# Recurrence products of 64x64 cut into 32x32, and their compact results half as wide

## The chip, the cores and the metric

The kernel runs on one NeuronCore of a Trainium2 chip (trn2). The metric is the device time of one execution in microseconds, here the median of three runs. The engines are TensorE (PE in the profile, its weight loads PEld), VectorE (DVE), ScalarE (ACT), GpSimd (POOL) and SyncE (SP, which issues the DMAs of the weights).

## What is computed

Two blocks of a network on 256 tokens of width 2048 in float32: a convolution mixer, a gated linear recurrence (HGRN2), sliding window attention and a SwiGLU. The change touches the recurrence alone. For each of 16 heads of 128 channels and for both directions it computes, with `b` the running sum of the log forget gates:

```
diff = b[:, :, :, None, :] - b[:, :, None, :, :]
decay = jnp.exp(jnp.where(lower_tri, diff, -jnp.inf))
scores = jnp.einsum("bhtk,bhsk,bhtsk->bhts", qb, kb, decay)
o_intra = jnp.einsum("bhts,bhsv->bhtv", scores, vb)
```

The decay depends on query, key and channel, so the scores aren't one matrix product.

## The kernel before

All large products are three passes in fp32r (high part times high part and two cross terms, lines 508 to 510). Weights stream through four slots: SP loads a chunk of 256x512, ACT rounds it (`w_hi`, L761), DVE or POOL computes the rest (`w_lo`, L1146), PE multiplies 12 times. A tick is one chunk on each engine, and the other work is hooked behind ticks by hand (`Hooks`). Every engine runs its list strictly in order; semaphores join them (`g_mm` counts PE's levels, `g_G` the finished operands, `g_S` the taken results).

The recurrence splits the 256x256 score matrix of a head into a diagonal and off-diagonal squares of halving size: `LEVELS = [64, 32, 16, 8, 4, 2, 1]`. Within one square the decay factors into a part of the query and a part of the key relative to a boundary between them, so a level is an ordinary product of two scaled operands. Four heads form a group (`j` = 0 to 3), and there are nine steps `s`: 0 the diagonal, 1 the square of 128, 2 to 8 the seven levels. For each step:

- `diffs` (DVE, lines 1355 to 1358) writes the exponents to `E`, `exp` (ACT, L959) takes their exponential, `weigh` (DVE, L1366) multiplies by the query;
- `level` (PE) multiplies. Before, it computes for each of four heads and two token blocks two 64x64 squares on the diagonal of a 128x128 block, and in step 2 the two squares beside it. In steps 3 to 8 most of a 64x64 square is not wanted: the squares of the level lie inside it;
- `take` gets the wanted entries out of PSUM (`T`) into SBUF: `SB` is a compact array of the squares, `ST` the full 128x128 blocks. Steps 0 to 3 are taken by ACT, 4 to 8 by DVE with a copy under the mask `lmask` (L1375).

At the end `blocks` (ACT, L988) puts `SB` into the diagonal of `ST`, and `av` (PE, lines 624 and 625) multiplies the scores by the values. PE runs the steps of group `j` between the chunks of the next weights: step 0 after tick 8, step 1 after 13, step `s` after 10 + 2 s, `av` after 28. DVE and ACT have their parts of them one tick later, which is earlier in time, since they run ahead of PE. After the last step of a group DVE transposes the next group's gates in quarters, POOL moves the quarters (L448, `kf`, `kb`, `qT`), ACT makes gates of them.

Of the kernel before, what the change touches and what calls it, by code (L numbers as in the profile page):

```python
# [29 lines left out]
I32 = mybir.dt.int32  # L30
ACT = mybir.ActivationFunctionType
# [3 lines left out]
P = 128  # L35
D = 2048
S = 256
# [12 lines left out]
HPG = GC // P  # L50
# [7 lines left out]
LEVELS = [64, 32, 16, 8, 4, 2, 1]  # L58
TWO_PI = 2 * np.pi
QUARTER = P // 4  # L60
LN_MIN = 2.0 ** -64
FIRST_LOWS = 2 * CPG
ACT_TAKES = 4
HB = P // 2
# [68 lines left out]
def is_first(j):  # L133
    return isinstance(j, int) and j == 0
# [19 lines left out]
def build(nc, t, out):  # L154
    ph = phases()
    ctx = ExitStack()
    with ctx:
        def sb(stack, name, shape, dt=F32):
            return stack.enter_context(nc.sbuf_tensor(name, shape, dt))

        def sem(name):
            return ctx.enter_context(nc.semaphore(name))
# [19 lines left out]
        mix = ExitStack()  # L182
        y_hi = sb(mix, "y_hi", [P, KT, S], F32R)
        ones = sb(mix, "ones", [P, P])
        lmask = sb(mix, "lmask", [P, len(LEVELS) + 2 - ACT_TAKES, P // 2], I32)
        wmask = sb(mix, "wmask", [P, 3 * P])
        inv_freq = sb(mix, "inv_freq", [P, HD // 2])
        onorm = sb(mix, "onorm", [P, P])
# [21 lines left out]
        hs = ExitStack()  # L210
# [7 lines left out]
        qT = sb(hs, "qT", [P, HPG, S])  # L218
# [3 lines left out]
        Xc = sb(hs, "Xc", [P, HPG, S])  # L222
        E = sb(hs, "E", [P, 2, 2, HPG, S])
        ST = sb(hs, "ST", [P, 2, HPG, 2, P])
        SB = sb(hs, "SB", [P, HPG, 2, P // 2])
        back = sb(hs, "back", [P, 2, HPG])
        ssh = sb(hs, "ssh", [P, 3, 2 * HPG])
        powers = sb(hs, "powers", [P, 2 * HPG])
# [29 lines left out]
        T = ctx.enter_context(nc.psum_tensor("T", [P, 4, 512], F32))  # L258
# [3 lines left out]
        def gate_banks(k):  # L262
# [17 lines left out]
        g_raw, g_q, g_M, g_act, g_lb, g_D, g_E, g_G, g_mm, g_S = (  # L280
            sem(f"hgrn_{s}") for s in ("raw", "quarters", "moved", "act", "lb", "D", "E", "G", "mm", "S"))
# [202 lines left out]
        def _(pe):  # L484
# [48 lines left out]
            def v_turn(j):  # L533
                if is_first(j):
                    pe.wait_ge(small_in, 16)
                pe.wait_ge(c_v, j + 1)
                if not is_first(j):
                    pe.wait_ge(c_pad, 2 * j)
                transposes(T01, atok, c_T)
# [43 lines left out]
            at = Hooks().put(4, lambda: v_turn(3))  # L583
# [11 lines left out]
            def level(j, s):  # L595

                pe.wait_ge(g_G, 9 * j + s + 1)
                if s == 0:
                    pe.wait_ge(g_M, 3 * j + 3)
                if s >= 2:  # L600
                    pe.wait_ge(g_S, 9 * j + s - 1)
                e = E[:, (s + 1) % 2, :, :, :]
                for h in range(HPG):
                    for b in range(2):
                        if s == 1:
                            last = nc.tensor.matmul(T[:, h // 2, (h % 2) * S + b * P:(h % 2) * S + b * P + P],
                                                    e[:, 0, h, b * P:(b + 1) * P], e[:, 1, h, (1 - b) * P:(2 - b) * P],
                                                    start=True, stop=True)
                            continue
                        for i in range(2):  # L610
                            at = (2 * b + i) * HB
                            to = (2 * b + 1 - i) * HB if s == 2 else at
                            g, q = (e[:, 1, h, at:at + HB], qT[:, h, to:to + HB]) if s == 0 else (e[:, 0, h, at:at + HB], e[:, 1, h, to:to + HB])
                            last = nc.tensor.matmul(T[i * HB:(i + 1) * HB, 2 + s % 2, (2 * h + b) * HB:(2 * h + b + 1) * HB],
                                                    g, q, start=True, stop=True)
                last.then_inc(g_mm, 1)

# [10 lines left out]
            def process(j):  # L628

                at = Hooks().put(8, lambda: level(j, 0))  # L630
                for s in range(1, 9):
                    at.put(13 if s == 1 else 10 + 2 * s, lambda s=s: level(j, s))
                return at.put(28, lambda: av(j))
# [18 lines left out]
            at = process(3)  # L652
# [59 lines left out]
            at = Hooks().put(14, k_turn)  # L712
            for g in range(4):
                e = 16 + 8 * g
# [23 lines left out]
        def _(act):  # L738
            A = nc.scalar.activation
# [84 lines left out]
            def v_steps(j):  # L824
                return Hooks().put(2, lambda: b_out(j)).put(4 if j < 2 else 6, lambda: pad_copy(j))
# [25 lines left out]
            def z_out(k):  # L851
                if k:
                    act.wait_ge(c_zT, k)
                evacuate("conv_z", 0, k, 0, sg, ACT.Silu, c_z)

            def z_copy(k):
                act.wait_ge(c_zT, k + 1)
                for b in range(2):
                    A(szt[:, 4 * k + 2 * b:4 * k + 2 * b + 2, :].rearrange("p a b -> p (a b)"), T[:, b, :],
                      ACT.Copy).then_inc(c_zc, 1)  # L860
# [20 lines left out]
            def ln_act(u):  # L881
                act.wait_ge(c_n, u + 1)
                for kt in (2 * u, 2 * u + 1):
                    last = A(cy[:, kt, :], cy[:, kt, :], ACT.Silu, scale=feat[:, kt, R_LNG:R_LNG + 1], bias=feat[:, kt, R_LNB:R_LNB + 1])
                last.then_inc(c_act, 1)
# [5 lines left out]
            at = v_steps(3)  # L891
# [8 lines left out]
            at = Hooks().put(0, lambda: ln_act(0)).put(3, lambda: z_out(3)).put(5, lambda: z_copy(3))  # L900
# [60 lines left out]
            def take(j, s):  # L961

                act.wait_ge(g_mm, 9 * j + s + 1)
                if s == 0:
                    A(SB[:, :, :, :].rearrange("p a b c -> p (a b c)"), T[:, 2, :], ACT.Copy).then_inc(g_S, 1)
                    return
                if s == 1:
                    if not is_first(j):
                        act.wait_ge(g_av, j)
                    A(ST[:, 0, :, :, :].rearrange("p a b c -> p (a b c)"), flat(T01), ACT.Copy).then_inc(g_S, 1)  # L970
                    return
                c = LEVELS[s - 2]
                ps = T[:, 2 + s % 2, :].rearrange("p (a c) -> p a c", c=HB)
                for i in range(P // c):
                    r, o = slice(i * c, (i + 1) * c), (i ^ 1) * c
                    if s == 2:
                        last = A(ST[r, 1, :, :, o:o + c].rearrange("p a b c -> p (a b) c"), ps[r, :, :], ACT.Copy)
                    else:
                        o = o % HB
                        last = A(SB[r, :, :, o:o + c].rearrange("p a b c -> p (a b) c"), ps[r, :, o:o + c], ACT.Copy)  # L980
                last.then_inc(g_S, 1)

            def blocks(j):

                act.wait_ge(g_S, 9 * j + 9)
                for i in range(2):
                    r = slice(i * HB, (i + 1) * HB)
                    last = A(ST[r, 1, :, :, i * HB:(i + 1) * HB].rearrange("p a b c -> p (a b) c"),  # L988
                             SB[r, :, :, :].rearrange("p a b c -> p (a b) c"), ACT.Copy)
                last.then_inc(g_sb, 1)  # L990

# [41 lines left out]
            at = Hooks().put(3, lambda: raw_out(3, 3, vtok)).with_(process(3)).with_(rest(2))  # L1033
# [54 lines left out]
            at = Hooks()  # L1088
            for g in range(-1, 4):
                e = 16 + 8 * g  # L1090
# [34 lines left out]
        def _(dve):  # L1125
# [103 lines left out]
            at = Hooks()  # L1229
# [42 lines left out]
            at = Hooks()  # L1272
# [95 lines left out]
            def take(j, s):  # L1368

                settle()  # L1370
                if s == ACT_TAKES:
                    dve.wait_ge(g_S, 9 * j + s)
                dve.wait_ge(g_mm, 9 * j + s + 1)
                V.memset(none[:, :], 0.0)
                V.copy_predicated(SB[:, :, :, :].rearrange("p a b c -> p (a b) c"),  # L1375
                                  lmask[:, s - ACT_TAKES, :].unsqueeze(1).to_broadcast([P, 8, HB]),
                                  T[:, 2 + s % 2, :].rearrange("p (a c) -> p a c", c=HB)).then_inc(g_S, 1)

            def o_norm(j):
                dve.wait_ge(g_o, 2 * (j + 1))  # L1380
# [57 lines left out]
            at = process(3).with_(rest(2))  # L1438
# [133 lines left out]
            at = Hooks()  # L1572
            for g in range(-1, 4):
                e = 16 + 8 * g
# [39 lines left out]
            at = Hooks().put(2, lambda: u_out(FJ - 1)).put(3, lambda: f_quarters(FJ - 1)).put(13, lambda: f_lo_out(FJ - 1))  # L1614
# [6 lines left out]
def constants():  # L1621

    i = np.arange(P)
    k, q = i[:, None] % HB, i[None, :HB]
    levels = np.stack([(k // (2 * c) == q // (2 * c)) & (k // c != q // c) for c in LEVELS[ACT_TAKES - 2:]], 1).astype(np.int32)
    q, k = i[:, None], i[None]
    allowed = np.concatenate([k <= q, k > q, k <= q], 1)
    wmask = np.where(allowed, 0.0, -1e30).astype(np.float32)
    inv = (np.float32(10000.0) ** (-np.arange(0, HD, 2, dtype=np.float32) / np.float32(HD))).astype(np.float32)
    return {"c_ident": np.eye(P, dtype=np.float32), "c_lmask": levels, "c_wmask": wmask, "c_inv_freq": inv[None]}  # L1630
# [36 lines left out]
```

## Time and profile before

| | |
|---|---|
| median of 3 runs | 1934.54 us (1933.37 to 1935.49) |
| the profiled execution's own time | 1934.93 us |
| its span | 1933.1 us |
| granted clock of TensorE | 1.00 |
| PE, DVE, ACT, POOL busy | 99%, 67%, 56%, 29% |
| the recurrence of the four groups | some 488 to 868 us |

A busy share is an average over stages with different limits. The time of a record is its own, and records of one engine overlap: a matmul of 0.39 us is followed by the next after 0.23. A float32 product such as those of `level` is two records of PE.

### The profile page before, as it was taken

How to read it: one execution, taken by the hardware profiler on the slowest of the kernel's cores; microseconds unless marked ns; L12 is line 12 of the kernel's file. 1: busy time of each engine (PE TensorE's matmuls, PEld its weight loads, DVE VectorE, ACT ScalarE, POOL GpSimd, SP SyncE). 2: the span in 40 equal slices, each digit the busy share in tenths (PEclk: the TensorE clock that was granted, in tenths of full speed). 3: DMA queues.
4: the chain of work that ended last, by engine and by line, in shares of the span. 5: the costliest groups of instructions: out<-in, count | busy, mean ns of one | idle time of the engine just before them, and what ended most of it. 6: DMA issues, size and time to landing. Idle time of an engine off the chain costs nothing.

```text
span 1933.1 us, 26528 instructions
## 1 busy us (share of the span) xinstructions
PE 1918.3 (99%) x9668; PEld 1573.9 (81%) x9668; DVE 1302.0 (67%) x1852; ACT 1075.4 (56%) x1405; POOL 555.6 (29%) x616
## 2 busy tenths in 40 slices
PE   7999999999999999999999999999999999999999
PEld 6888878888888888888887778888888888888887
DVE  5799967556878888886667877555555555554443
ACT  6444466456768686875467775544444444443332
POOL 0899852306050423302400106023222222220000
PEclk9999999999999999999999999999999999999999
DMA  8666656666555555555654445666666666666665
GB/s 298 198 188 189 181 163 194 187 197 185 163 165 163 147 180 152 174 150 179 195 186 134 129 145 180 199 195 195 193 190 192 191 196 191 193 194 195 192 193 161
DMA packets 183006, 352.45 MB, mean 182 GB/s; under 512 B 11776, under 2 KB 12288, under 8 KB 182912
## 3 DMA queue, kind: packets, MB, share of 16 engines
q1 hardware_dynamic: 181488, 350.68, 60.1%
q8 instruction: 57, 0.93, 0.2%
q10 hardware_dynamic: 1424, 0.53, 0.1%
q14 instruction: 37, 0.30, 0.0%
HBM read 349.07 MB, written 2.10 MB: 182 GB/s over the span
## 4 chain that ended last, share of the span: by engine, by line
PE 79%; issue 6%; DVE 4%; ACT 4%; POOL 4%; DVEq 1%; POOLq 1%; ACTq 0%; DMA 0%
PE acc L508 26%; PE acc L510 25%; PE acc L509 25%; POOL kb L448 2%; POOL kf L448 1%; ACT E L959 1%; DVEq L1132 1%; DVE w_lo L1146 1%; PE T L490 1%; ACT w_hi L761 1%; PE T L709 1%; PE T L698 1%; POOLq L443 0%; DVE E L1366 0%; DVE E L1358 0%
## 5 line engine op out<-in xcount | busy, mean ns | idle before, releaser
L1146 DVE TENSOR_TENSOR w_lo<-raw,w_hi 128x1024 fp32r<-128x1024 f32 x568 | 699.1, 1234 | 538.3 <-ACT w_hi L761 530.7
L761 ACT ACTIVATE w_hi<-raw 128x1024 fp32r<-128x1024 f32 x656 | 688.4, 1057 | 601.3 <-PE acc L510 577.9
L508 PE MATMUL acc<-w_hi,h_hi 128*128 128x512 f32 x1888 | 745.2, 395 | 9.9 <-DVE w_lo L1146 9.7
L510 PE MATMUL acc<-w_hi,h_lo 128*128 128x512 f32 x1888 | 736.8, 390 | 0.0
L509 PE MATMUL acc<-w_lo,h_hi 128*128 128x512 f32 x1888 | 736.8, 390 | 0.0
L508 PEld LDWEIGHTS acc<-w_hi,h_hi 128*128 128x128 f32 x1888 | 355.3, 188 | 89.8 <-issue 14.2
L510 PEld LDWEIGHTS acc<-w_hi,h_lo 128*128 128x128 f32 x1888 | 355.2, 188 | 74.4
L509 PEld LDWEIGHTS acc<-w_lo,h_hi 128*128 128x128 f32 x1888 | 355.5, 188 | 71.2
L479 POOL COPY fT<-fq 32x256 f32<-32x256 f32 x176 | 110.8, 630 | 388.2 <-DVE fq L1599 381.3
L417 POOL TENSOR_TENSOR w_lo<-raw,w_hi 128x1024 fp32r<-128x1024 f32 x80 | 190.3, 2404 | 76.4 <-ACT w_hi L761 76.3
L1219 DVE SCALAR_TENSOR_TENSOR T<-vpad,feat,T 128x256 f32<-128x256 f32 x464 | 182.4, 478 | 0.0
L508 PE MATMUL acc<-w_hi,y_hi 128*128 128x512 f32 x384 | 151.5, 395 | 1.3 <-DVE hy_lo L1151 1.1
L509 PE MATMUL acc<-w_lo,y_hi 128*128 128x512 f32 x384 | 149.6, 390 | 0.0
L510 PE MATMUL acc<-w_hi,f_lo 128*128 128x512 f32 x352 | 137.0, 389 | 0.0
L508 PE MATMUL acc<-w_hi,f_hi 128*128 128x512 f32 x352 | 137.0, 389 | 0.0
L509 PE MATMUL acc<-w_lo,f_hi 128*128 128x512 f32 x352 | 137.0, 389 | 0.0
L448 POOL COPY kf<-sz 32x256 f32<-32x256 f32 x64 | 37.2, 581 | 289.6 <-DVEq L1132 287.1
L510 PE MATMUL acc<-w_hi,hy_lo 128*128 128x512 f32 x256 | 99.8, 390 | 0.0
L508 PEld LDWEIGHTS acc<-w_hi,y_hi 128*128 128x128 f32 x384 | 72.1, 188 | 17.6 <-DVE hy_lo L1151 1.4
L509 PEld LDWEIGHTS acc<-w_lo,y_hi 128*128 128x128 f32 x384 | 72.2, 188 | 14.4
L959 ACT ACTIVATE E<-E 128x2048 f32<-128x2048 f32 x28 | 53.7, 1917 | 43.5 <-DVE E L1358 43.4
L510 PEld LDWEIGHTS acc<-w_hi,f_lo 128*128 128x128 f32 x352 | 66.1, 188 | 13.8
(237 smaller groups left out, 1564.2 us busy)
## 6 DMA issues: line engine op xcount, KB each, us to landing
raw<-in_hgrn_w_in_dram SPq DMA_DIRECT2D x160, 512.0 KB, 3.7
raw<-in_conv_w_in_dram SPq DMA_DIRECT2D x96, 512.0 KB, 4.2
raw<-in_ffn_w_gate_dram SPq DMA_DIRECT2D x88, 512.0 KB, 4.4
raw<-in_ffn_w_up_dram SPq DMA_DIRECT2D x88, 512.0 KB, 4.5
raw<-in_ffn_w_down_dram SPq DMA_DIRECT2D x88, 512.0 KB, 4.8
raw<-in_attn_w_qkv_dram SPq DMA_DIRECT2D x40, 512.0 KB, 4.1
raw<-in_conv_w_out_dram SPq DMA_DIRECT2D x32, 512.0 KB, 4.6
raw<-in_hgrn_w_out_dram SPq DMA_DIRECT2D x32, 512.0 KB, 4.6
```

Of the source, the lines that this page charges most:

```text
L417: nc.gpsimd.tensor_tensor(w_lo[:, slot, :, :], raw[:, slot, :, :], rounded(w_hi[:, slot, :, :]), ALU.subtract).then_inc(split_ready, 1)
L448: last = nc.gpsimd.tensor_copy(turned_block(dst, a, b), own_block(src, a, b))
L479: last = nc.gpsimd.tensor_copy(turned_block(fT, a, b), own_block(fq, a, b))
L490: last = nc.tensor.transpose(dst[:, q // 2, at:at + P], src[:, tb, q * P:(q + 1) * P], ident[:, :])
L508: nc.tensor.matmul(o, hi[:, kt, a], w_hi[:, slot, kk, :], start=kt == 0, stop=False)
L509: nc.tensor.matmul(o, hi[:, kt, a], w_lo[:, slot, kk, :], start=False, stop=False)
L510: last = nc.tensor.matmul(o, lo[:, kt, a], w_hi[:, slot, kk, :], start=False, stop=kt == p.chunks * CK - 1)
L698: last = nc.tensor.transpose(T[:, h % 2, b * P:(b + 1) * P], sm[:, h, (b + 1) * P:(b + 2) * P], ident[:, :])
L761: A(w_hi[:, slot, :, :], raw[:, slot, :, :], ACT.Copy).then_inc(hi_ready, 1)
L959: A(e, e, ACT.Exp).then_inc(g_E, 1)
L1146: TT(w_lo[:, slot, :, :], raw[:, slot, :, :], rounded(w_hi[:, slot, :, :]), ALU.subtract).then_inc(split_ready, 1)
L1219: STT(out=cy[:, kt, :] if tap == TAPS - 1 else y, in0=v, scalar=w, in1=y, op0=ALU.mult, op1=ALU.add).then_inc(c_tap, 1)
```

## The change

Products of 64x64 become products of 32x32 in step 0 and in steps 3 to 8. Step 0 computes four 32x32 squares on the diagonal of a 128x128 block. Step 3 (squares of 32) computes exactly the four wanted squares beside the diagonal, and ACT copies them straight to `ST`. Steps 4 to 8 compute the four diagonal squares, and their wanted parts go to an `SB` and through a mask that are 32 wide in place of 64. Step 2 keeps its 64x64 products. `blocks` copies four quarters in place of two halves.

```diff
--- before.py
+++ after.py
@@ -182,7 +182,7 @@
         mix = ExitStack()
         y_hi = sb(mix, "y_hi", [P, KT, S], F32R)
         ones = sb(mix, "ones", [P, P])
-        lmask = sb(mix, "lmask", [P, len(LEVELS) + 2 - ACT_TAKES, P // 2], I32)
+        lmask = sb(mix, "lmask", [P, len(LEVELS) + 2 - ACT_TAKES, QUARTER], I32)
         wmask = sb(mix, "wmask", [P, 3 * P])
         inv_freq = sb(mix, "inv_freq", [P, HD // 2])
         onorm = sb(mix, "onorm", [P, P])
@@ -222,7 +222,7 @@
         Xc = sb(hs, "Xc", [P, HPG, S])
         E = sb(hs, "E", [P, 2, 2, HPG, S])
         ST = sb(hs, "ST", [P, 2, HPG, 2, P])
-        SB = sb(hs, "SB", [P, HPG, 2, P // 2])
+        SB = sb(hs, "SB", [P, HPG, 2, QUARTER])
         back = sb(hs, "back", [P, 2, HPG])
         ssh = sb(hs, "ssh", [P, 3, 2 * HPG])
         powers = sb(hs, "powers", [P, 2 * HPG])
@@ -607,11 +607,12 @@
                                                     e[:, 0, h, b * P:(b + 1) * P], e[:, 1, h, (1 - b) * P:(2 - b) * P],
                                                     start=True, stop=True)
                             continue
-                        for i in range(2):
-                            at = (2 * b + i) * HB
-                            to = (2 * b + 1 - i) * HB if s == 2 else at
-                            g, q = (e[:, 1, h, at:at + HB], qT[:, h, to:to + HB]) if s == 0 else (e[:, 0, h, at:at + HB], e[:, 1, h, to:to + HB])
-                            last = nc.tensor.matmul(T[i * HB:(i + 1) * HB, 2 + s % 2, (2 * h + b) * HB:(2 * h + b + 1) * HB],
+                        n = HB if s == 2 else QUARTER
+                        for i in range(P // n):
+                            at = b * P + i * n
+                            to = b * P + (i ^ 1) * n if s in (2, 3) else at
+                            g, q = (e[:, 1, h, at:at + n], qT[:, h, to:to + n]) if s == 0 else (e[:, 0, h, at:at + n], e[:, 1, h, to:to + n])
+                            last = nc.tensor.matmul(T[i * n:(i + 1) * n, 2 + s % 2, (2 * h + b) * n:(2 * h + b + 1) * n],
                                                     g, q, start=True, stop=True)
                 last.then_inc(g_mm, 1)
 
@@ -962,7 +963,7 @@
 
                 act.wait_ge(g_mm, 9 * j + s + 1)
                 if s == 0:
-                    A(SB[:, :, :, :].rearrange("p a b c -> p (a b c)"), T[:, 2, :], ACT.Copy).then_inc(g_S, 1)
+                    A(SB[:, :, :, :].rearrange("p a b c -> p (a b c)"), T[:, 2, 0:S], ACT.Copy).then_inc(g_S, 1)
                     return
                 if s == 1:
                     if not is_first(j):
@@ -970,22 +971,18 @@
                     A(ST[:, 0, :, :, :].rearrange("p a b c -> p (a b c)"), flat(T01), ACT.Copy).then_inc(g_S, 1)
                     return
                 c = LEVELS[s - 2]
-                ps = T[:, 2 + s % 2, :].rearrange("p (a c) -> p a c", c=HB)
+                ps = T[:, 2 + s % 2, 0:2 * HPG * c].rearrange("p (a c) -> p a c", c=c)
                 for i in range(P // c):
                     r, o = slice(i * c, (i + 1) * c), (i ^ 1) * c
-                    if s == 2:
-                        last = A(ST[r, 1, :, :, o:o + c].rearrange("p a b c -> p (a b) c"), ps[r, :, :], ACT.Copy)
-                    else:
-                        o = o % HB
-                        last = A(SB[r, :, :, o:o + c].rearrange("p a b c -> p (a b) c"), ps[r, :, o:o + c], ACT.Copy)
+                    last = A(ST[r, 1, :, :, o:o + c].rearrange("p a b c -> p (a b) c"), ps[r, :, :], ACT.Copy)
                 last.then_inc(g_S, 1)
 
             def blocks(j):
 
                 act.wait_ge(g_S, 9 * j + 9)
-                for i in range(2):
-                    r = slice(i * HB, (i + 1) * HB)
-                    last = A(ST[r, 1, :, :, i * HB:(i + 1) * HB].rearrange("p a b c -> p (a b) c"),
+                for i in range(4):
+                    r = slice(i * QUARTER, (i + 1) * QUARTER)
+                    last = A(ST[r, 1, :, :, r].rearrange("p a b c -> p (a b) c"),
                              SB[r, :, :, :].rearrange("p a b c -> p (a b) c"), ACT.Copy)
                 last.then_inc(g_sb, 1)
 
@@ -1373,8 +1370,8 @@
                 dve.wait_ge(g_mm, 9 * j + s + 1)
                 V.memset(none[:, :], 0.0)
                 V.copy_predicated(SB[:, :, :, :].rearrange("p a b c -> p (a b) c"),
-                                  lmask[:, s - ACT_TAKES, :].unsqueeze(1).to_broadcast([P, 8, HB]),
-                                  T[:, 2 + s % 2, :].rearrange("p (a c) -> p a c", c=HB)).then_inc(g_S, 1)
+                                  lmask[:, s - ACT_TAKES, :].unsqueeze(1).to_broadcast([P, 8, QUARTER]),
+                                  T[:, 2 + s % 2, 0:S].rearrange("p (a c) -> p a c", c=QUARTER)).then_inc(g_S, 1)
 
             def o_norm(j):
                 dve.wait_ge(g_o, 2 * (j + 1))
@@ -1621,7 +1618,7 @@
 def constants():
 
     i = np.arange(P)
-    k, q = i[:, None] % HB, i[None, :HB]
+    k, q = i[:, None] % QUARTER, i[None, :QUARTER]
     levels = np.stack([(k // (2 * c) == q // (2 * c)) & (k // c != q // c) for c in LEVELS[ACT_TAKES - 2:]], 1).astype(np.int32)
     q, k = i[:, None], i[None]
     allowed = np.concatenate([k <= q, k > q, k <= q], 1)
```

On PE, the instructions around step 4 of the first group before the change: lines 508 to 510 are the weight stream, L614 the products of `level` (shape of the result, number).

```order
L508 MATMUL acc<-w_hi,h_hi 128x512
L509 MATMUL acc<-w_lo,h_hi 128x512
L510 MATMUL acc<-w_hi,h_lo 128x512
L614 MATMUL T<-E 64x64 [waits hgrn_S,hgrn_G]
L614 MATMUL T<-E 64x64 x15
L508 MATMUL acc<-w_hi,h_hi 128x512 [waits split_ready]
```

The same place in the changed kernel (`level` now lies one line further down):

```order
L508 MATMUL acc<-w_hi,h_hi 128x512
L509 MATMUL acc<-w_lo,h_hi 128x512
L510 MATMUL acc<-w_hi,h_lo 128x512
L615 MATMUL T<-E 32x32 [waits hgrn_S,hgrn_G]
L615 MATMUL T<-E 32x32 x31
L508 MATMUL acc<-w_hi,h_hi 128x512 [waits split_ready]
```

The place and the waits are the same; 16 products have become 32 of a quarter of the size.

On DVE, the instructions between the `diffs` of one step and those of the next, before the change; each waits for PE (`hgrn_mm`) or ACT (`hgrn_E`, `hi_ready`) as shown:

```order
L1146 TENSOR_TENSOR w_lo<-raw,w_hi 128x1024 [waits hi_ready]
L1374 MEMSET none 128x2 [waits hgrn_mm]
L1375 COPY_PREDICATED SB<-lmask,T 128x512
L1366 TENSOR_TENSOR E<-E,qT 128x1024 [waits hgrn_E]
L1146 TENSOR_TENSOR w_lo<-raw,w_hi 128x1024 [waits hi_ready]
```

In the changed kernel:

```order
L1143 TENSOR_TENSOR w_lo<-raw,w_hi 128x1024 [waits hi_ready]
L1371 MEMSET none 128x2 [waits hgrn_mm]
L1372 COPY_PREDICATED SB<-lmask,T 128x256
L1363 TENSOR_TENSOR E<-E,qT 128x1024 [waits hgrn_E]
L1143 TENSOR_TENSOR w_lo<-raw,w_hi 128x1024 [waits hi_ready]
```

Only the size of the masked copy has changed. No instruction has moved on any engine.

## Rows read from the trace of the kernel before

**Rows 1.** The profile page, its head and part 1: busy time (share) xinstructions.
```profile
span 1933.1 us, 26528 instructions
PE 1918.3 (99%) x9668; PEld 1573.9 (81%) x9668; DVE 1302.0 (67%) x1852; ACT 1075.4 (56%) x1405; POOL 555.6 (29%) x616
```

**Rows 2.** Waits of PE's weight loads, whole execution: total us, times, longest.
```profile
PEld T L614 <- DVE E L1366: 4.9, 14, 0.4
PEld acc L508 <- DVE w_lo L1146: 2.1, 6, 0.6
```

**Rows 3.** Timeline of PE, 527 to 536: start, duration (us), instructions.
```profile
527.91 1.15 PE L614 MATMUL T<-E 128*64 128x64 f32 x32
528.99 0.50 PE L508 MATMUL acc<-w_hi,h_hi 128*128 128x512 f32 x1
...
534.66 1.15 PE L614 MATMUL T<-E 128*64 128x64 f32 x32
```

**Rows 4.** Timeline of DVE, 526 to 534.
```profile
526.25 1.23 DVE L1366 TENSOR_TENSOR E<-E,qT 128x1024 f32<-128x1024 f32 x1
...
530.34 0.68 DVE L1358 TENSOR_TENSOR E<-Bc 128x512 f32<-128x512 f32 x1
530.94 1.22 DVE L1146 TENSOR_TENSOR w_lo<-raw,w_hi 128x1024 fp32r<-128x1024 f32 x1
532.28 0.76 DVE L1375 COPY_PREDICATED SB<-lmask,T 128x512 f32<-128x512 int32 x1
533.01 1.23 DVE L1366 TENSOR_TENSOR E<-E,qT 128x1024 f32<-128x1024 f32 x1
```

**Rows 5.** Timeline of ACT, the same stretch.
```profile
531.06 1.92 ACT L959 ACTIVATE E<-E 128x2048 f32<-128x2048 f32 x1 [2.94 <-DVE E L1358]
```

**Rows 6.** Timelines of GpSimd (POOL) and of ACT between the first two groups.
```profile
550.20 9.78 POOL L448 COPY kf<-sz 32x256 f32<-32x256 f32 x16 [69.94 <-DVEq L1132]
567.17 9.10 POOL L448 COPY kb<-aftok 32x256 f32<-32x256 f32 x8 [0.15 <-issue]
...
576.38 1.06 ACT L923 ACTIVATE qtok<-kb 128x1024 f32<-128x1024 f32 x1 [3.13 <-POOL kb L448]
```

**Rows 7.** Timelines of DVE and of PE's weight loads at 585.
```profile
584.41 1.42 DVE L1146 TENSOR_TENSOR w_lo<-raw,w_hi 128x1024 fp32r<-128x1024 f32 x1
...
585.88 0.19 PEld L508 LDWEIGHTS acc<-w_hi,h_hi 128*128 128x128 f32 x1 [0.55 <-DVE w_lo L1146]
```

**Rows 8.** Waits of all engines: the one of level 1's take.
```profile
ACT ST L970 <- PE T L606: 4.1, 4, 3.1
```

**Rows 9.** Stretches, instructions on T alone: us, PE busy (x), PEld busy (x), others.
```profile
232.38:232.42 0.04, 0.03 (x4) 0.03 (x5) 0.04 (x1) 0.00 (x0) 1.00 0.00 0
488.23:488.26 0.03, 0.02 (x2) 0.02 (x2) 0.00 (x0) 0.00 (x0) 1.00 0.56 205
```

**Rows 10.** Lines: count, duration ns min/median/max, first and last start, shapes.
```profile
L614 PE MATMUL T<-E x896: 221/222/271, 507.7 to 858.9; 128*64 128x64 f32 x180
L564 PE MATMUL T<-cy,ones x32: 378/380/404, 232.4 to 259.7; 128*32 128x256 f32 x32
```

**Rows 11.** Timelines: PE at 232, PE and ACT at 864.
```profile
232.39 1.50 PE L564 MATMUL T<-cy,ones 128*32 128x256 f32 x24
...
864.64 0.38 PE L624 MATMUL T<-vtok,ST 128*128 128x128 f32 x2
...
862.75 1.27 ACT L988 ACTIVATE ST<-SB 64x512 f32<-64x512 f32 x2 [2.15 <-DVE SB L1375]
```

**Rows 12.** Lines of ACT, as in rows 10.
```profile
L980 ACT ACTIVATE SB<-T x16: 355/376/380, 516.0 to 827.0; 32x256 f32<-32x256 f32 x16
L988 ACT ACTIVATE ST<-SB x8: 629/630/632, 552.6 to 863.4; 64x512 f32<-64x512 f32 x8
```

**Rows 13.** Timelines of DVE and PE at the last level of the first group.
```profile
546.53 1.23 DVE L1366 TENSOR_TENSOR E<-E,qT 128x1024 f32<-128x1024 f32 x1
...
548.15 1.15 PE L614 MATMUL T<-E 128*64 128x64 f32 x32
```

## The prediction

> **What bounds the kernel now.** I read the page first [rows 1]: TensorE (PE) is busy 99% of the span, VectorE (DVE) 67%, ScalarE (ACT) 56%. That says "the matmul stream is the bound", and would price every nanosecond taken off PE at one nanosecond of the kernel. The second view, the waits of PE's weight loads [rows 2], seems to agree: before L614, the products that the change narrows, it shows 14 gaps of 0.35 us put down to the DVE product before them, and 6 short waits for `w_lo` in the whole execution.
>
> The third view is the timeline of the recurrence (some 488 to 868 us), and it changes the reading. PE starts one level at 527.91 and the next at 534.66, a period of 6.75 us [rows 3]. DVE's `weigh` (L1366), without whose result the level can't start, runs at 526.25 and 533.01, a period of 6.76 us, and DVE has no gap in between [rows 4]. So two chains of equal length run side by side. The second one holds no PE instruction: `weigh`, `w_lo`, four `diffs` on DVE, `exp` on ACT, `weigh` again. The last `diffs` ends at 530.34 + 0.68 = 531.02, `exp` runs from 531.06 to 532.98 [rows 5], `weigh` starts at 533.01. The take (copy_predicated, L1375) that the change halves runs in the shadow of `exp`: 532.28 + 0.76 = 533.04 [rows 4].
>
> The chain goes on between two groups of heads: after the last `weigh` come DVE's transposes, then GpSimd moves `kf` from 550.20 and the second half of `kb` from 567.17 to 576.27, ACT takes up `kb` at 576.38 after 3.13 us of waiting [rows 6], and through ACT and DVE this ends in a `w_lo` that is done at 584.41 + 1.42 = 585.83. PE starts on it at 585.88, after 0.55 us without a weight load [rows 7]. That is one hand-over, 0.05 us: here PE has no lead at all. Only in the first group does PE lead: of ACT's four waits for level 1, 4.1 us in all, the first group's is the long one of 3.1 [rows 8].
>
> **The change part by part.**
>
> Products on PE. In each group levels 0 and 3 to 8, seven in all, go from 16 products of 64x64 to 32 of 32x32; level 2 stays. One product is two records of the profile, so a level goes from 32 to 64 records. What paces them: in 0.03 us at the start of a level two records on T start together, and at the start of L564, whose outputs cycle over four 32-partition quarters, four do [rows 9]. So products for different column groups of the array run side by side: in sets of two records now, and of four in the changed code, whose inner loop cycles over four quarters. A level now is 16 sets: 1.15 - 0.22 = 0.93 us from first to last start, 0.062 us a step over 15 steps [rows 3, 10]. L564 is 6 sets at 256 columns: 1.50 - 0.38 = 1.12 us, 0.224 a step over 5 steps [rows 10, 11]. The slope is 162 ns over 192 columns, 0.84 ns a column, so a step at 32 columns is 62 - 27 = 35 ns. The changed level is again 16 sets, so 15 x 0.035 = 0.53 us: 0.40 us less. Times 7 levels and 4 groups: 11.2 us of PE work go. This is an estimate for a shape that the trace doesn't have. The far ends: the sets stay pairs (31 steps of 0.035 = 1.09 us, 0.16 more than now, +4.5 us in all), or records can't follow one another faster than in the quickest long run of this trace, 0.93/31 = 0.030 us each (63 x 0.030 = 1.89 us, 0.96 more a level, +27 us). I take the middle reading, since four together in 0.04 us is a row of this trace and nothing in it shows a limit at 0.030.
> The Trainium skill has a rule against this change: "TensorE: Matmul & The Clock Gate", section "Wait — 56ns, not 53.3ns?", says that matmuls, start to start, never come closer than about 25 ns however few columns they have. By that rule 64 records would want 63 x 0.025 = 1.58 us, 0.65 more a level and 18 us in all. The starts side by side in [rows 9] disagree with it as a limit on single starts; that it holds for a long run of narrow products no row here excludes.
>
> DVE's takes. Five per group at 0.76 us for 512 elements [rows 4] get 256; between 0.38 (half) and 0.76 (all fixed), I take 0.46. Four of the five lie under `exp`, so they return nothing: once the take ends earlier, `exp` (532.98) is what `weigh` waits for. The fifth, before `blocks`, gives 0.3 us to ACT.
>
> ACT. Level 0's copy halves (ACT waits there anyway). Level 3 keeps its four copies of 32x256 and only writes to ST. `blocks` goes from two copies of 64x512 at 0.63 to four of 32x256, priced at level 3's 0.376 [rows 12]: 1.27 against 1.50 us, 0.23 more. That eats the fifth take's 0.3. No DMA, queue or wait is added; the mask table loaded once at the start is half as big.
>
> Where the 11.2 us go. PE is early, and in a strict order it waits at the next thing that the other chain hands it.
> - First group, level 0: PE leads here, 0.40 us is real, and the chain behind it, fed by level 1, also moves 0.40 earlier.
> - Levels 3 to 8: `weigh` of level 8 ends at 546.53 + 1.23 = 547.76 and the level starts at 548.15 [rows 13]. Less the hand-over of 0.05, PE can start 0.34 us earlier than now and no more. Levels 3 to 7 have given 2.0 us, so 1.7 of them become waits for L1366.
> - Level 8 itself: 0.40 more. At `av` the first group is 0.40 + 0.34 + 0.40 = 1.14 us ahead.
> - Next group: the chain over GpSimd is only 0.40 ahead (it hung on `weigh`, not on PE), so at the place of 585.88 PE falls back to 0.40. The same holds for the second and third crossing: nothing adds up from group to group. Level 0 of groups 2 to 4 is lost likewise to the `w_lo` and `weigh` that follow it.
> - Fourth group: again 1.14 us ahead at the end of level 8. There `av` needs `blocks`, which wait 2.15 us for the take and end at 862.75 + 1.27 = 864.02, with `av` at 864.64 [rows 11, 12]. It moves 0.40 + 0.30 - 0.23 = 0.47 earlier, so `av` can be 0.47 + 0.57 = 1.04 ahead. What follows (ScalarE's output copies, the norm, the z projection) hangs on `av` and passes it on.
>
> Sum: 1.0 us, against the profiled execution's own 1934.93 us; its span of 1933.1 would be 1932.1. The median of the three runs is 1934.54, 0.4 below the profiled one, so I forecast 1933.5.
>
> **The rivals.** A measurement of this kernel can tell about 0.2% (3.9 us) from no change.
> - A, PE alone is the bound: all 11.2 us come back, 1923.3. For it: 99% busy. Against it: the equal periods [rows 3, 4] and the missing lead [rows 7]. For this DVE, ACT and GpSimd would have to have slack that the timeline doesn't show.
> - B, slower: pace of the records. If a long run of records is limited singly, PE, which has nothing to spare, adds each nanosecond 28 times. It decides from 0.14 us a level (28 x 0.14 = 3.9), that is, when 64 records need over 1.07 us from first to last start, 17 ns each. At 30 ns it gives 1961. By the rule of the Trainium skill quoted above it would be 1953.
> - C, the sets stay pairs: +0.16 a level, 28 times, 1939.0; for a mix of pairs and fours, at half of that, 1936.7.
> - D, the other chain itself gets longer or shorter by a few tenths per group: DVE's halved take disturbs GpSimd's `kf` moves less, four small copies cost more than priced, tables that lie at other addresses. It gives +-0.5 us a group, 1931.5 to 1935.5, and doesn't change the verdict.
>
> **How the numbers follow.** Forecast with D: 0.74, of which 0.01 below -0.2%. A: 0.07. B: 0.09. C: 0.07, of which 0.03 above 0.2%. The other chain longer by more than D allows: 0.03. Faster by over 0.2%: 0.08; within: 0.77; slower: 0.15. The predicted time is the likeliest case's, 1933.5. The range 1931.0 to 1938.0 holds forecast and D and half of C, 0.77 to 0.8; A and B are outside it.
>
> **What the changed profile should show.** L615 with 64 records per narrowed level, some 0.75 us long in place of 1.15, and the stream's next matmul 0.7 instead of 1.08 us after the level's first. Level starts in the late levels still 6.75 us apart, with waits for DVE's `weigh` of 0.35 + 0.4 us. PE's wait for `w_lo` at the group crossings about 0.7 us longer than 0.3. `weigh` now with a short gap before it put down to ACT. Group period still 103 us. Were I wrong, the level periods would fall to 6.35 (A) or rise above 6.9 (B, C).

## The result and the profile after

Seventeen runs of each kernel side by side: 1934.95 us before (1933.37 to 1936.67) and 1938.58 us after (1937.33 to 1941.68). The ratio is 1.002, 95% interval 1.0013 to 1.0027. The forecast was 1933.5 with a range up to 1938.0. The changed kernel is some 3.6 us slower, close to 0.2%, and outside the range.

The head of the changed kernel's page, which answers to [rows 1]:

```profile
span 1936.7 us, 28328 instructions
PE 1914.8 (99%) x10564; PEld 1563.9 (81%) x10564; DVE 1297.8 (67%) x1852; ACT 1076.7 (56%) x1413; POOL 556.5 (29%) x616
```

TensorE (PE) has 3.5 us less busy time in a span that is 3.6 us longer. The waits of PE and of its weight loads (total us, times, longest), which answer to [rows 2]:

```profile
PEld T L615 <- DVE E L1363: 13.1, 20, 0.8
PEld acc L508 <- DVE w_lo L1143: 5.2, 8, 1.2
PE T L615 <- DVE E L1363: 4.9, 16, 0.3
```

The waits of the weight loads for `weigh` grew by 8.2 us and those for `w_lo` by 3.1: together that is about the 11 us taken off PE, which are there again as waits. The timeline of PE and its weight loads at a late level, against [rows 3]:

```profile
528.41 0.76 PE L615 MATMUL T<-E 128*32 128x32 f32 x64 [0.29 <-DVE E L1363]
529.10 0.50 PE L508 MATMUL acc<-w_hi,h_hi 128*128 128x512 f32 x1
...
535.16 0.76 PE L615 MATMUL T<-E 128*32 128x32 f32 x64 [0.33 <-DVE E L1363]
...
528.41 0.65 PEld L615 LDWEIGHTS T<-E 128*32 128x32 f32 x64 [0.71 <-DVE E L1363]
```

A level is 0.76 us long in place of 1.15 and the stream goes on 0.69 us after its start in place of 1.08, but the next level still starts 6.75 us later. DVE and ACT in the same stretch, against [rows 4, 5]:

```profile
527.13 1.23 DVE L1363 TENSOR_TENSOR E<-E,qT 128x1024 f32<-128x1024 f32 x1 [0.21 <-ACT E L960]
...
531.21 0.69 DVE L1355 TENSOR_TENSOR E<-Bc 128x512 f32<-128x512 f32 x1
531.81 1.22 DVE L1143 TENSOR_TENSOR w_lo<-raw,w_hi 128x1024 fp32r<-128x1024 f32 x1
533.15 0.45 DVE L1372 COPY_PREDICATED SB<-lmask,T 128x256 f32<-128x256 int32 x1
533.88 1.23 DVE L1363 TENSOR_TENSOR E<-E,qT 128x1024 f32<-128x1024 f32 x1 [0.28 <-ACT E L960]
...
531.93 1.92 ACT L960 ACTIVATE E<-E 128x2048 f32<-128x2048 f32 x1 [2.95 <-DVE E L1355]
```

`weigh` to `weigh` is 6.75 us as before; the shorter take only leaves a gap of 0.28 us in front of `weigh`, and the gap ends with ACT's `exp`. So far everything is as forecast, and nothing here is longer than before. The loss is elsewhere.

To find it, I paired the L508 products of two traces by their number (2,624 are recorded in each) and took the difference of their starts (us, + is later), with product 80 as zero. The columns marked 1, 2, 7 and 8 belong to experiments told below.

| product, its time before | after | 1 | 2 | 7 | 8 |
|---|---|---|---|---|---|
| 400, 299 us (in conv_out) | +0.09 | -0.03 | +0.05 | -0.04 | +0.01 |
| 600, 436 us (behind conv_out) | +1.46 | +0.01 | +1.42 | 0.00 | +0.03 |
| 800, 589 us (first group done) | +1.08 | -0.41 | +1.41 | -2.70 | -0.19 |
| 1100, 832 us (fourth group) | +0.45 | -1.10 | +1.50 | -6.81 | -0.51 |
| 1300, 983 us (behind hgrn_out) | +2.51 | -0.68 | +3.15 | -8.31 | -0.51 |
| 1500, 1164 us (in att_out) | +2.75 | -0.66 | +3.41 | -8.28 | -0.49 |
| 1600, 1233 us (behind att_out) | +3.65 | -0.66 | +4.31 | -8.28 | -0.49 |
| 2600, 1913 us | +3.65 | -0.66 | +4.31 | -8.28 | -0.49 |

In the recurrence the changed kernel gains up to 1.0 us (+1.46 to +0.45), of which some 0.6 is left behind its last `av` (+0.88 at product 1152). It loses in three streams that the diff doesn't touch: conv_out, hgrn_out and att_out. These are the streams whose second stationary part is `y_lo` or `hy_lo`. The answer for the line of the low product, L510 in both kernels (duration in ns, min/median/max), in the changed kernel:

```profile
L510 PE MATMUL acc<-w_hi,h_lo x1888: 387/389/628, 10.7 to 1693.3; 128*128 128x512 f32 x189
L510 PE MATMUL acc<-w_hi,f_lo x352: 388/389/389, 1693.9 to 1932.6; 128*128 128x512 f32 x176
L510 PE MATMUL acc<-w_hi,hy_lo x256: 389/397/401, 880.7 to 1213.6; 128*128 128x512 f32 x128
L510 PE MATMUL acc<-w_hi,y_lo x128: 387/397/401, 287.6 to 376.7; 128*128 128x512 f32 x128
```

The same instruction takes 8 ns more where it reads `y_lo` or `hy_lo`. These tensors lie behind the mask table in SBUF. The narrower table moves them down by 640 bytes per partition, from byte 144,512 to 143,872, that is, from remainder 128 to remainder 0 by 256. The weights `w_hi` and `w_lo` and the parts `h_hi`, `h_lo`, `y_hi`, `f_hi`, `f_lo` have remainder 128 in both kernels.

### The profile page after: what moved, and what is told of

Same layout as the page of the kernel before. It is cut to its first block, busy times and chain, and to the rows that moved or that the text cites. A ratio compares the mean times of both kernels' runs of the same rounds, so it can differ in the third digit from the quotient of the medians.

```text
span 1936.7 us, 28328 instructions
## 1 busy us (share of the span) xinstructions
PE 1914.8 (99%) x10564; PEld 1563.9 (81%) x10564; DVE 1297.8 (67%) x1852; ACT 1076.7 (56%) x1413; POOL 556.5 (29%) x616
## 4 chain that ended last, share of the span: by engine, by line
PE 79%; issue 6%; ACT 4%; DVE 4%; POOL 4%; DVEq 1%; POOLq 1%; ACTq 0%; DMA 0%
PE acc L508 25%; PE acc L509 25%; PE acc L510 25%; POOL kb L448 2%; ACT E L960 2%; POOL kf L448 1%; DVEq L1129 1%; DVE w_lo L1143 1%; PE T L490 1%; ACT w_hi L762 1%; PE T L710 1%; PE T L699 1%; DVE E L1363 0%; DVE E L1353 0%; DVE E L1354 0%
## 5 line engine op out<-in xcount | busy, mean ns | idle before, releaser
L508 PE MATMUL acc<-w_hi,h_hi 128*128 128x512 f32 x1888 | 745.4, 395 | 11.8 <-DVE w_lo L1143 11.7
L510 PE MATMUL acc<-w_hi,h_lo 128*128 128x512 f32 x1888 | 736.3, 390 | 0.0
L508 PEld LDWEIGHTS acc<-w_hi,h_hi 128*128 128x128 f32 x1888 | 355.1, 188 | 92.4 <-issue 14.1
L510 PEld LDWEIGHTS acc<-w_hi,h_lo 128*128 128x128 f32 x1888 | 355.1, 188 | 75.1
L508 PE MATMUL acc<-w_hi,y_hi 128*128 128x512 f32 x384 | 151.3, 394 | 1.2 <-DVE hy_lo L1148 1.1
L508 PE MATMUL acc<-w_hi,f_hi 128*128 128x512 f32 x352 | 136.9, 389 | 0.0
L510 PE MATMUL acc<-w_hi,f_lo 128*128 128x512 f32 x352 | 136.9, 389 | 0.0
L510 PE MATMUL acc<-w_hi,hy_lo 128*128 128x512 f32 x256 | 101.6, 397 | 0.0
L508 PEld LDWEIGHTS acc<-w_hi,y_hi 128*128 128x128 f32 x384 | 73.5, 191 | 19.2 <-DVE hy_lo L1148 1.3
L509 PEld LDWEIGHTS acc<-w_lo,f_hi 128*128 128x128 f32 x352 | 66.1, 188 | 13.8
```

The source lines that it names most:

```text
L508: nc.tensor.matmul(o, hi[:, kt, a], w_hi[:, slot, kk, :], start=kt == 0, stop=False)
L509: nc.tensor.matmul(o, hi[:, kt, a], w_lo[:, slot, kk, :], start=False, stop=False)
L510: last = nc.tensor.matmul(o, lo[:, kt, a], w_hi[:, slot, kk, :], start=False, stop=kt == p.chunks * CK - 1)
```

## Experiments

Theory M (for the memory address) says that this move costs the time, R that the changed instructions do. Runs 1 to 4 are compared with one set of runs of the kernel before, 5 to 8 with a second, 9 and 10 with a single run. "Kernel 1" below is the changed kernel with the gap of experiment 1.

**1. The tables put back.**

```
         lmask = sb(mix, "lmask", [P, len(LEVELS) + 2 - ACT_TAKES, QUARTER], I32)
+        sb(mix, "gap", [P, 160])
```

> The changed kernel with 640 unused bytes per partition behind the mask table, so that every tensor allocated behind it (y_lo, hy_lo, the tensors of the recurrence up to ST) lies again at the address that it has in the kernel before; nothing else is changed. Theory M (the loss is not in the recurrence: with y_lo and hy_lo at another address the low products of the three output streams start 232 to 234 ns apart instead of 227): the pitches go back to 227, the three streams give back their 1.5 + 1.6 + 1.2 us, and the kernel takes 1934.3, some 0.6 below the kernel before, near the forecast's 1.0 less. Theory R (the narrower products, takes or block copies themselves cost the time, the addresses being a bystander): no change, 1938.6.

Measured: 1934.24 us (1933.04 to 1935.63), ratio 0.9997 to the kernel before (0.9988 to 1.0006). The low products of the changed kernel with the gap:

```profile
L511 PE MATMUL acc<-w_hi,hy_lo x256: 387/389/397, 880.4 to 1210.5; 128*128 128x512 f32 x128
L511 PE MATMUL acc<-w_hi,y_lo x128: 387/389/398, 288.9 to 376.5; 128*128 128x512 f32 x128
```

And twelve products of conv_out by the timeline, first in the changed kernel, then in this one:

```profile
330.29 0.40 PE L510 MATMUL acc<-w_hi,y_lo 128*128 128x512 f32 x1
...
333.06 0.40 PE L510 MATMUL acc<-w_hi,y_lo 128*128 128x512 f32 x1
```

```profile
330.23 0.39 PE L511 MATMUL acc<-w_hi,y_lo 128*128 128x512 f32 x1
...
332.95 0.39 PE L511 MATMUL acc<-w_hi,y_lo 128*128 128x512 f32 x1
```

Twelve products take 2.77 us there and 2.72 here. Column 1 of the table no longer rises in any of the three streams. 640 unused bytes give 4.3 us back; R falls.

**2. The kernel before, its tensors moved.**

```
         lmask = sb(mix, "lmask", [P, len(LEVELS) + 2 - ACT_TAKES, P // 2], I32)
+        sb(mix, "gap", [P, 96])
```

> The kernel before with 384 unused bytes per partition behind its mask table. All instructions are those of the kernel before; y_lo and hy_lo lie at an address that has the same remainder as the changed kernel's by 1024 (512), though not the same address. Theory M, if the remainder is what counts: 4.3 us slower than the kernel before, 1939.2, with L509 to L510 some 232 ns and L510 to L508 some 234 ns apart. Theory R: no change, 1934.9.

Measured: 1939.05 us (1937.37 to 1940.66), ratio 1.0021 (1.0012 to 1.0031). Column 2 rises by 1.4, 1.65 and 1.25 us in the same three streams (the last from +3.05 at product 1440, where att_out begins) and by nothing that matters in the recurrence. So the loss needs nothing of the changed instructions.

**3 and 4. Other places.** Gaps of other sizes in front of `y_lo`, of the tensors of the recurrence with `hy_lo`, and of `f_lo`, in the changed kernel:

```
+        sb(conv_s, "gap_y", [P, 32])     # run 4: 224
         y_lo = sb(conv_s, "y_lo", [P, KT, S], F32R)
...
+        sb(mix, "gap_h", [P, 64])        # run 4: 16
         hs = ExitStack()
...
+        sb(ctx, "gap_f", [P, 8])         # run 4: 96
         f_lo = sb(ctx, "f_lo", [P, FKT, S], F32R)
```

> The changed kernel with small gaps in front of three tensors, to find which addresses are slow: y_lo at remainder 640 by 1024 (128 by 512), hy_lo at 768 (256 by 512, 0 by 256), f_lo at 672 (160 by 256; 640 in both kernels so far). Read is the distance of starts in each stream. Theory M with a period of 512: conv_out at 227, hgrn_out and att_out possibly in between or slow, gate_up and down changed only if a shift of 32 bytes counts. With a period of 1024 (only 128 and, for f_lo, 640 fast by chance) conv_out would stay at 232 to 234. Theory R: no stream changes its distances.

> As the kernel with the first set of gaps, with other places: y_lo at remainder 384 by 1024 (384 by 512, 128 by 256), hy_lo at 576 (64 by 512), f_lo at 0 by 1024 (0 by 512). Theory M: f_lo at 0 slows the streams gate_up and down, which no kernel so far did, to 232 to 234 ns for their low products, some 12 ns per pair of low products; conv_out is at 227 if the period is 256, and at 232 or more if it is 512; hy_lo shows whether 64 bytes count as 128 do. Theory R: gate_up and down keep 227.

**5 and 6. Everything, or the weights alone, 128 bytes on.** From kernel 1, one gap in front of `raw` (5), or one in front of `w_hi` and one in front of `h_hi` (6), which moves the weights by 128 and everything from `h_hi` on by 256:

```
# run 5
+        sb(ctx, "gap_all", [P, 32])
         raw = sb(ctx, "raw", [P, SLOTS, CK, GC])
# run 6
+        sb(ctx, "gap_w", [P, 32])
         w_hi = sb(ctx, "w_hi", [P, SLOTS, CK, GC], F32R)
...
+        sb(ctx, "gap_h", [P, 32])
         h_hi = sb(ctx, "h_hi", [P, KT, S], F32R)
```

> The changed kernel with its tables put back (640 bytes), and 128 unused bytes in front of all tensors: weights, h, y and f all move together from remainder 128 by 256 to remainder 0. Theory M-absolute (a stationary part at remainder 0 by 256 is slow, wherever the moving part lies): every low product of every stream pays some 12 ns, some 2,700 of them, at least 30 us more, 1965 or above. Theory M-relative (only a difference between the addresses of the weights and of the stationary part is slow): all distances stay at 227 ns and the kernel takes 1934. Theory R has no place for a change of time here either.

> The changed kernel with its tables put back, and the weights w_hi and w_lo 128 bytes further on, at remainder 0 by 256, while all stationary parts (h, y, f) keep the remainder 128. Theory M-absolute: stationary parts are where they are fast, distances stay at 227, 1934. Theory M-relative: weights and stationary parts differ by 128 as in the three slow streams, so every stream slows, 1965 or above.

**9 and 10. w_lo alone, and three more distances.** Also from kernel 1. Run 9 has the first gap of run 6 in front of `w_lo` instead of `w_hi`; run 10 has gaps of 32, 64 and 192 bytes where runs 3 and 4 have theirs.

> The changed kernel with its tables put back, and of the weights only w_lo 128 bytes further on, at remainder 0 by 256; w_hi and all stationary parts keep remainder 128. The stationary part of L511 (h_lo, y_lo, f_lo) is loaded while L510 streams w_lo. If what counts is the address that is streamed while another is loaded, only L510 to L511 should be 232 instead of 227, some 5.5 ns 2,700 times or 14 us, 1949. If the moving part's own address against that of the stationary part it meets counts, L509 to L510 or L510 to L511 alone or both are slow, up to 28 us.

> The changed kernel with its tables put back and three small gaps: y_lo 32 bytes, hy_lo 64 bytes and f_lo 192 bytes off the remainder that the weights have by 256. Theory M-relative: all three of their streams are slower than 227 ns; y_lo by as much as f_lo was when it was 32 bytes off (239 from L510 to L511), the two others by an amount that fills the table. If only the distance counts and not its sign, 64 and 192 (64 to the other side) give the same.

What the six showed. The times are of one run each: 1943.9 (3), 1941.1 (4), 1934.7 (5), 1968.7 (6), 1970.8 (9), 1945.2 (10), beside 1934.2 to 1935.1 for the kernel before. The median distances between starts inside a stream, in ns, worked out from the records, in the order high product, product with `w_lo`, product with the low part, next high product ("off" is the low part's address less that of the weights, by 256). The last column is the mean of the three steps together, over rounds that nothing interrupts (each step under 250 ns); for `hy_lo` it is that of hgrn_out:

| stationary low part (run) | off | high to w_lo | w_lo to low | low to high | all three |
|---|---|---|---|---|---|
| y_lo (before, 1), hy_lo (before, 1), f_lo (before) | 0 | 226-227 | 226-227 | 226-227 | 680-681 |
| y_lo at 512 and at 256 bytes on from before (3, 4, modulo 1024) | 0 | 227 | 226-227 | 226-227 | 680-681 |
| all tensors at remainder 0 (5) | 0 | 226-227 | 226-227 | 226-227 | 680-681 |
| y_lo, hy_lo (after, 2) | 128 | 227 | 232-233 | 234 | 694 |
| hy_lo (3), f_lo (4) | 128 | 227 | 232-233 | 234 | 693-694 |
| f_lo (3) | 32 | 233 | 239 | 228 | 700 |
| y_lo (10) | 32 | 233 | 239 | 228 | 700 |
| hy_lo (10) | 64 | 228 | 229 | 236 | 693 |
| f_lo (10) | 192 | 228 | 232 | 235 | 693 |
| hy_lo (4) | 192 | 227 | 232 | 231 | 693 |
| weights apart from all parts (6), h | 128 | 232 | 232 | 232 | 697 |
| w_lo apart from w_hi and all parts (9), h | 0 to w_hi | 236 | 234 | 230 | 698 |

Run 3's `y_lo`, 512 bytes on, at 227 rules out that only one place in 1024 bytes is fast, and run 4's, 256 bytes on, that only one in 512 is. The two large losses are seen in the products' mean duration on the page, here the low product of the main streams in runs 6 and 9:

```profile
L513 PE MATMUL acc<-w_hi,h_lo 128*128 128x512 f32 x1888 | 746.0, 395 | 0.0
```

```profile
L513 PE MATMUL acc<-w_hi,h_lo 128*128 128x512 f32 x1888 | 742.7, 393 | 0.0
```

against a mean of 390 in run 5. Run 5 rules out M-absolute: nothing is slow at remainder 0 when everything is there. Run 6 confirms M-relative, with +34 us for 128 bytes. Both readings tried in run 9 fell: they gave 14 to 28 us, and it is 36.6; not one or two steps got slower but all three. Run 10's `y_lo` repeats run 3's `f_lo` step for step, so 32 bytes cost the same in two different streams. 64 and 192 bytes off spread their loss over other steps, but all three steps together take 693 ns in both, as with 128 (693 to 694): some 13 ns a round at 64, 128 and 192, some 20 at 32. (The medians of the steps mislead at 192: the two rows differ by 4 ns in the last median, but the means of their steps are alike, 229, 231 and 234 ns.)

**7 and 8. The diffs ahead of w_lo.** In VectorE's order, in kernel 1 (7) and in the kernel before (8):

```
-                        at.put(12 + 2 * s, lambda s=s: diffs(j, s + 1))
+                        at.put(11 + 2 * s, lambda s=s: diffs(j, s + 1))
```

> The changed kernel with its tables put back, and on VectorE the four diffs of the next level put right behind weigh, ahead of the w_lo that stood between them. The chain weigh, diffs, exp, weigh then has no w_lo in it: 1.14 + 2.41 + 1.95 = 5.5 us plus hand-overs, in place of 6.74. The forecast's theory (TensorE's 11 us are freed but hidden by that chain): the levels' period falls from 6.75 to what comes next, VectorE's own work of 6.47 with a take and TensorE's 6.35 without, some 2 us a group and 8 us in all, 1926 to 1928. Rival H (the freed time is no time of TensorE's: something else, such as the weights' arrival, holds the period at 6.75): no change, 1934.2. Rival W (w_lo now comes too late for the second chunk of a level): slower than 1934.2.

> The same move of the diffs in the kernel before. The forecast's theory: TensorE alone needs the whole 6.75 us here, and VectorE with its take of 0.76 us needs 6.77, so nothing is gained, 1934 to 1935.5; the difference to the same move in the changed kernel is then what the narrower products and takes are worth once the chain is out of the way. Rival (the gain of the move has nothing to do with the change): this kernel gets faster by as much as the changed one.

Measured: 1926.74 us (1925.44 to 1927.60), ratio 0.9957 (0.9943 to 0.9971) for 7; 1934.80 (1933.52 to 1936.60), ratio 0.9998 (0.9989 to 1.0007) for 8. The timeline of 7, PE and then DVE:

```profile
527.43 0.76 PE L616 MATMUL T<-E 128*32 128x32 f32 x64
...
533.81 0.76 PE L616 MATMUL T<-E 128*32 128x32 f32 x64
...
525.57 1.22 DVE L1364 TENSOR_TENSOR E<-E,qT 128x1024 f32<-128x1024 f32 x1
526.70 0.69 DVE L1353 TENSOR_TENSOR E<-Bc,kf 128x512 f32<-128x512 f32 x1
...
529.11 2.35 DVE L1144 TENSOR_TENSOR w_lo<-raw,w_hi 128x1024 fp32r<-128x1024 f32 x2
...
531.59 0.46 DVE L1373 COPY_PREDICATED SB<-lmask,T 128x256 f32<-128x256 int32 x1
531.93 1.21 DVE L1364 TENSOR_TENSOR E<-E,qT 128x1024 f32<-128x1024 f32 x1
```

And of 8:

```profile
530.10 1.15 PE L614 MATMUL T<-E 128*64 128x64 f32 x32
...
536.84 1.15 PE L614 MATMUL T<-E 128*64 128x64 f32 x32
...
528.06 1.22 DVE L1366 TENSOR_TENSOR E<-E,qT 128x1024 f32<-128x1024 f32 x1
...
534.09 0.77 DVE L1375 COPY_PREDICATED SB<-lmask,T 128x512 f32<-128x512 int32 x1
534.74 1.21 DVE L1366 TENSOR_TENSOR E<-E,qT 128x1024 f32<-128x1024 f32 x1
```

The levels are 6.38 us apart in 7 and 6.74 in 8, in both with no wait in front of them, and `weigh` follows the take at once: it starts 6.36 us after the one before in 7 and 6.68 in 8. So `exp` is no longer what is waited for; what is left is the two engines' own work, and that is what the change makes shorter. The same move is worth 7.6 us by the table after the change (-8.28 against -0.66) and 0.5 us before it. H (something else holds the period) and W (`w_lo` comes too late) fall. What is left of waits shows in the waits of PE's weight loads between 480 and 880 us, in 7 and then in 8:

```profile
PEld acc L509 <- DVE w_lo L1144: 3.8, 9, 0.8
```

```profile
PEld acc L508 <- DVE w_lo L1146: 1.1, 4, 0.3
```

Kernel 7 has 2.7 us more of them. Paired product by product, its lead over 8 falls by 0.15, 0.7 and 0.7 us at the three crossings and by some 0.35 us behind each level 0 of groups 2 to 4, together 2.7 us. That is what it doesn't return: 7.8 us kept and 2.7 lost are the 10.5 that the 28 narrowed levels gave. That these waits are the cause fits the numbers but was not tried by a run of its own. Kernel 7 is the fastest of all, 8 us below the kernel before and 12 below the changed one.

## Why the prediction was wrong, and where it was right

**The step that failed** is the account of what the change moves. It named "tables that lie at other addresses" in rival D as one of three causes of +-0.5 us a group in the recurrence, gave it no price of its own, and the sum put nothing outside the recurrence; of the mask table it said only that it is half as big. What the half table costs is 4.3 us, in three streams with 384 low products: by the distances some 5.4 + 7 ns each, 4.8 us. That the 0.5 between the two went into waits that were there anyway is likely (att_out, where 24 of 128 rounds are interrupted, loses 1.3 us; hgrn_out, with 5, loses 1.65), but not shown. Nothing in the rows ahead of the prediction could price it, but the diff shows the shape of an allocation, and the streams make up most of the span: the range should have allowed for it. The kernel before even holds a hint. Behind its tables, right in front of `y_lo`, stand 160 unused bytes, `sb(mix, "align_low", [P, 40])`; without them `y_lo` would lie at 144,352, which is remainder 224, and with them it lies at 128 like the weights. The change took 640 bytes away ahead of this padding and left the padding as it was. The changed kernel less kernel 1 (column "after" less column 1) goes from -0.03 to 1.49 us in conv_out, from 1.54 to 3.19 in hgrn_out and from 3.05 to 4.31 in att_out, products 384 to 512, 1152 to 1280 and 1440 to 1568. The 4.31 minus kernel 1's gain of 0.66 is the whole of the +3.65.

**Equal chains** was right. The freed 11 us turned into waits for `weigh` and `w_lo`, the period stayed at 6.75, and runs 7 and 8 show the other side: with `w_lo` out of the chain the change is worth 7.8 us (8.28 - 0.49), with it, 0.66. Rival A falls.

**Sets of four** was right, and B and C fall: 64 records take 0.76 - 0.20 = 0.56 us from first to last start, against an estimate of 0.53, and 0.39 us less a level against 0.40. These are the lines of the changed kernel, as in [rows 10, 12]:

```profile
L615 PE MATMUL T<-E x1664: 196/196/270, 508.6 to 859.2; 128*32 128x32 f32 x171, 128*64 128x64 f32 x14
L985 ACT ACTIVATE ST<-SB x16: 412/416/418, 553.1 to 864.7; 32x256 f32<-32x256 f32 x16
L1372 DVE COPY_PREDICATED SB<-lmask,T x20: 446/451/455, 526.5 to 863.0; 128x256 f32<-128x256 int32 x20
```

That is 9 ns a record. The starts within the level at 528.41 show the sets: the first 32 records come in fours, the second to the eighth set 53, 84, 116, 148, 179, 211 and 243 ns behind the first, one every 32 ns against the estimate of 35; the rest come mostly in pairs, one every 15 to 17 ns. The rule of the Trainium skill ("TensorE: Matmul & The Clock Gate", section "Wait — 56ns, not 53.3ns?") of some 25 ns between starts does not hold for a run of products that cycle over the four quarters of the columns. Each quarter gets 16 of the 64 records, one every 35 ns on average, and no run here has narrow products on one quarter only, so for a single quarter the rule is not excluded.

**Where the 11.2 us go** was right step by step. The same pairing of L508 products, each time at which the lead of kernel 1 over the kernel before changes in the recurrence (product, its time before, difference in us):

```
676   489.3  -0.38    level 0, first group
708   515.5  -0.75    first of levels 3 to 8
716   522.2  -1.11
796   585.9  -0.41    first crossing
804   592.6  -0.80    level 0, second group
820   603.6  -0.41    back again
844   625.7  -1.16    levels of the second group
924   689.2  -0.35    second crossing
1052  792.4  -0.33    third crossing
1100  832.1  -1.10    levels of the fourth group
1140  868.1  -0.66    behind av of the fourth group
```

The forecast had 0.40 for level 0, 1.14 ahead of `av`, 0.40 behind each crossing, nothing that adds up. Only where the lead of the levels arises differs: it is full with the second narrowed level and stays, since the waits come with the levels behind it.

**The sum** of 1.0 us was a third too large, by its last step: 1.04 forecast behind `av`, 0.66 measured. The take was priced at 0.46 and took 0.451. The four `blocks` copies were priced by level 3's 0.376 and took 0.416 each. By the timeline of ACT and PE in the changed kernel, against [rows 11]:

```profile
863.44 1.69 ACT L985 ACTIVATE ST<-SB 32x256 f32<-32x256 f32 x4 [1.86 <-DVE SB L1372]
...
865.18 0.49 PE L625 MATMUL T<-vtok,ST 128*128 128x128 f32 x2
865.51 0.39 PE L626 MATMUL T<-vtok,ST 128*128 128x128 f32 x2
```

they cost 1.69 - 1.27 = 0.42 more in place of 0.23, while the wait for the last take fell by 0.29 as forecast, and `av` starts 0.05 us behind their end. That is 0.19 of the missing 0.38 us. The traces show the rest too. In kernel 1, whose product 80 starts 0.99 us later on its trace's clock than before, `blocks` start at 863.11 against 862.75 before, which is 0.63 earlier in place of the forecast 0.70. And the second pair of `av` starts 0.33 us behind the first (865.18 to 865.51; 0.32 in kernel 1) where it was 0.22 before (864.64 to 864.86); why, no run shows. Together that is nearly all of it. Level 3's own copies, which the term was read from, have the same shape but another source, T in place of SB.

**What stays open.** In every case tried, 227 ns were reached in all three steps only where the weights and all stationary parts share their remainder by 256 bytes; the remainders tried are multiples of 32. Why one part that is off also slows the step behind it (234 ns from a low product at remainder 0 to a high one at 128, over weights at 128) and why `w_lo` alone slows all three steps, the runs don't show. No kernel had the high part alone off.

## What to carry to other kernels

Before a diff is priced, print the address of every tensor in both versions: an edit that resizes one buffer moves all behind it, and here that cost more than the edit was worth. If the same instruction on another tensor has another duration, compare the addresses first. And where two chains of equal length run side by side, shortening one returns nothing until the other is shortened: look for work that sits inside the chain without belonging to it, as `w_lo` did between `weigh` and `diffs`, and for the slack that the change makes room for it.

## What the runs showed of the hardware

Back-to-back fp32r products of 128x512 with a new stationary part each start 227 ns apart when the stationary part and the weights have the same remainder by 256 bytes (0 or 128 for all, both tried), and in every other case tried (32, 64, 128 and 192 bytes off) one or more of the three steps takes 229 to 239 ns, and the three together 693 to 700 in place of 680 to 681; a whole kernel with a remainder of 128 between them is 34 us (1.8%) slower. The Trainium skill's page "SBUF — State Buffer", section "Operand start alignment", asks only for a multiple of the element's size and says of itself that it is about legality, not speed; all addresses here satisfy it. Float32 products of 128x32 over 32 columns that cycle over four column quarters start a record every 9 ns, which is a product (two records) every 18.
